# A third buffer for readout weights, a mask added by VectorE, spread bias loads and earlier modulation products in a two-layer hybrid backbone

## The reference

```python
sh1, sc1, g1, sh2, sc2, g2 = split(silu(c) @ w_mod[layer] + b_mod[layer], 6)   # modulation
h = modulate(rmsnorm(x, norm1_g[layer]), sh1, sc1)
...
states = associative_scan(combine, (lam_bar, bu))                              # state-space layer
y = einsum('blgp,ghp->blgh', states, c_re + 1j * c_im).real                    # readout
...
s_loc = einsum('bqhd,bikhd->bhqik', q_row, kb) * scale + bias[None]            # neighbourhood
s_loc = where(col_mask, s_loc, -inf)
p = softmax(concatenate([s_loc, s_ctx]))
...
y = gated_merge([glu(ssm), gqa, na], gates, w_branch, w_out)
```

## Time and profile before

| what | value |
| --- | --- |
| median of 3 runs | 2015.82 us (2014.27 to 2015.94) |
| the profiled execution | 2010.74 us |
| its span, first to last instruction | 2009.1 us |
| TensorE busy | 1714.0 us, 85% |
| VectorE busy | 637.3 us, 32% |
| ScalarE busy | 409.3 us, 20% |
| GpSimdE busy | 347.9 us, 17% |
| mean granted TensorE clock | 0.923 of full speed |

### The profile page before, as it was taken

How to read it: one execution, slowest core, us unless ns; L and a number is a source line. 1 busy time by engine, 2 the same in 40 slices (tenths; PEclk the granted TensorE clock), 3 DMA queues, 4 the chain that set the end, 5 groups by cost and what they waited for, 6 DMA issues and landing times.

```text
span 2009.1 us, 25439 instructions
## 1 busy us (share of the span) xinstructions
PE 1714.0 (85%) x9646; PEld 1049.6 (52%) x9646; DVE 637.3 (32%) x1378; ACT 409.3 (20%) x842; POOL 347.9 (17%) x284
## 2 busy tenths in 40 slices
PE   4999987899999998499979588998879994797794
PEld 1467554454444443355545336755458883464452
DVE  2578642351110113111101367774351112110012
ACT  3111211452000003122212231121242002121122
POOL 0004353681000000100000100435480000000000
PEclk8999986899999999699999788998789997899896
DMA  8411356508412125599999422145703427999992
GB/s 315 149 59 63 122 204 165 164 19 293 168 63 105 67 80 208 210 377 357 384 395 397 145 80 69 43 163 200 166 19 126 168 84 324 341 390 398 399 375 79
DMA packets 104882, 398.33 MB, mean 198 GB/s; under 512 B 43056, under 2 KB 52272, under 8 KB 64336
## 3 DMA queue, kind: packets, MB, share of 16 engines
q1 hardware_dynamic: 46960, 327.01, 41.9%
q10 hardware_dynamic: 50720, 29.54, 6.2%
q0 software_dynamic: 7104, 40.37, 5.9%
HBM read 370.67 MB, written 38.80 MB: 204 GB/s over the span
## 4 chain that ended last, share of the span: by engine, by line
PE 60%; DMA 14%; POOL 7%; DVE 6%; issue 5%; SPq 3%; ACT 3%; ACTq 1%; POOLq 0%; DVEq 0%
PE tile_ps L534 53%; DMA arena<-sorted_in 5%; PE turn_ps L534 4%; SPq L481 3%; DMA ring<-in_wpack 3%; POOL arena L1660 2%; DMA vn<-in_wpack 2%; DMA arena<-in_wpack 2%; PE out_ps L534 1%; DMA sorted_in<-arena,rows 1%; POOL arena L1654 1%; PE turn_ps L749 1%; ACTq L1045 1%; DVE rstd L1316 1%; POOL arena L1645 1%
## 5 line engine op out<-in xcount | busy, mean ns | idle before, releaser
L534 PE MATMUL tile_ps<-h,ring 128*128 128x512 f32 (+1 forms) x1312 | 475.3, 517 | 10.7 <-ACT h L930 8.0
L534 PEld LDWEIGHTS tile_ps<-h,ring 128*128 128x128 f32 x1312 | 250.6, 193 | 221.1 <-issue 206.0
L534 PE MATMUL tile_ps<-arena 64*16 64x128 f32 (+4 forms) x2032 | 244.2, 359 | 37.2 <-POOL arena L1645 16.5
L534 PE MATMUL tile_ps<-arena,ring 128*128 128x512 f32 (+1 forms) x704 | 235.3, 486 | 2.7 <-issue 2.7
L534 PEld LDWEIGHTS tile_ps<-arena 128*64 128x64 f32 (+3 forms) x2032 | 170.9, 161 | 94.1 <-issue 51.3
L534 PEld LDWEIGHTS tile_ps<-arena,ring 128*128 128x128 f32 x704 | 133.6, 190 | 96.6 <-issue 87.6
L1660 POOL TENSOR_SCALAR arena<-arena,smx 128x512 f32<-128x512 f32 (+1 forms) x96 | 127.9, 1349 | 86.8 <-DVE smx L1520 86.4
L534 PE MATMUL tile_ps<-ring,arena 128*64 128x256 f32 (+1 forms) x624 | 101.5, 469 | 9.9 <-ACT arena L1131 7.2
L1684 POOL DMA_DIRECT2D arena<-sorted_in x40 | 20.4, 511 | 515.7 <-PE tile_ps L834 515.7
L1112 ACT ACTIVATE arena<-tile_ps 128x512 f32<-128x512 f32 (+1 forms) x56 | 27.5, 491 | 347.4 <-PE tile_ps L534 347.4
L1581 DVE TENSOR_TENSOR arena<-tile_ps,arena 64x256 f32<-64x256 f32 x40 | 16.7, 417 | 228.2 <-ACT arena L1128 228.2
(11 more groups left out here) (258 smaller groups left out, 2157.2 us busy)
## 6 DMA issues: line engine op xcount, KB each, us to landing
ring<-in_wpack SPq DMA_DIRECT2D x176, 1024.0 KB, 7.9
arena<-in_wpack SPq DMA_DIRECT2D x64, 1024.0 KB, 28.8
h<-in_wpack SPq DMA_DIRECT2D x20, 1024.0 KB, 27.9
qa<-in_wpack SPq DMA_DIRECT2D x12, 1024.0 KB, 14.4
qn<-in_wpack SPq DMA_DIRECT2D x12, 1024.0 KB, 16.6
kn<-in_wpack SPq DMA_DIRECT2D x12, 1024.0 KB, 18.6
vn<-in_wpack SPq DMA_DIRECT2D x12, 1024.0 KB, 21.0
arena<-sorted_in POOLq DMA_DIRECT2D x42, 256.0 KB, 7.6
```

What stands on the lines that cost most here:

```text
L534: return nc.tensor.matmul(out, lhsT, rhs, start=start, stop=stop)
```

## The change

1. The readout weights get a third buffer, `q % 3`; GpSimdE waits for `y(q-3)`.
2. The `qn` projections of iterations 1, 2, 3, 4 go to iterations 1, 3, 5, 7.
3. Modulation blocks 0 and 1 of layer 1 go from attention steps 3 and 7 to iteration 8 of layer 0's readout loop, ahead of `y(7)`; blocks 2 and 3 go from steps 11 and 15 to steps 1 and 2.
4. The mask is added by VectorE in two parts of four additions each (128x512), at the end of steps 14 and 15 in layer 0, 6 and 7 in layer 1. GpSimdE's two additions go, and with them the wait at each masked pair.
5. ScalarE issues the bias loads of layer 0 in steps 0, 2, 4, 6 and the output loads in steps 8, 10, 12, 14; in layer 1 the bias loads stay in steps 0 to 3 and the output loads go to steps 4 to 7, one in each.

```diff
-EVERY = 4
+EARLY = {1: 2, 2: 3}
...
-    return fill[IN_LOOP:IN_LOOP + 2] if q == 0 else fill[IN_LOOP + 1 + q:IN_LOOP + 2 + q]
+    return [fill[IN_LOOP + n] for n, at in enumerate((0, 0, 1, 3, 5, 7)) if at == q]
...
+            names += mod_jobs(l + 1, range(2)) if q == NQ and l + 1 < LAYERS else []
...
+        cp = [cp_first, cp_second, cp_third]
...
+                    if q == NQ and l + 1 < LAYERS:
+                        for n in range(2):
+                            modulation(l + 1, n, l)
+                            modulation_columns(l + 1, n)
...
-                    if n < GRID_H:
-                        load_bias(l, n)
-                    if n == GRID_H:
+                    line = n // 2 if l == 0 and n % 2 == 0 else n if l else None
+                    if line in range(GRID_H):
+                        load_bias(l, line)
+                    if line in range(GRID_H, GRID_H + KW):
...
+                    part = n - len(us) // 2 + 2
+                    if 0 <= part < 2:
+                        dve.wait_ge(bias_in, 16 * GRID_H * (l + 1))
+                        for h2 in range(0, HEADS, 2):
+                            b = bias[:, part, h2:h2 + 2]
+                            b = b.rearrange("p h r c -> p (h r) c")
+                            link(TT(b, b, spread(c("far_cols"), 1, 2 * GRID_H), ALU.add))
...
-                    if q >= 2:
-                        wait_full(pool, (l, "yb", q - 2))
-                        wait_full(pool, (l, "y", q - 2))
+                    if q >= 3:
+                        wait_full(pool, (l, "yb", q - 3))
+                        wait_full(pool, (l, "y", q - 3))
...
-                    if n == 3 * len(us) // 8:
-                        pool.wait_ge(bias_in, 16 * GRID_H * (l + 1))
-                        for qt in range(2):
-                            b = bias[:, qt].rearrange("p h r c -> p (h r) c")
-                            TT(b, b, spread(c("far_cols"), 1, HEADS * GRID_H), ALU.add).then_inc(bias_done, 1)
```

More of the change, by code:

```diff
@@ L216, in tile_jobs @@
             names += [(l, "sc", u, 0), (l, "sc", u, 1)] if u < n_pairs else []
-            if l + 1 < LAYERS and u % EVERY == EVERY - 1 and u // EVERY < MOD1:
-                names += mod_jobs(l + 1, [u // EVERY])
+            names += mod_jobs(l + 1, [EARLY[u]]) if l + 1 < LAYERS and u in EARLY else []
         for kind, *at in mix_order():
@@ L331, in backbone @@
         wtmp, a1 = cut(a1, [GQ, STEP, GRP])
-        cp, a2 = cut(a0, [2, 2 * GQ, NPOS, GRP])
+        cp_first, a2 = cut(a0, [2, GQ, NPOS, GRP])
+        cp_second, a2 = cut(a2, [2, GQ, NPOS, GRP])
+        cp = [cp_first, cp_second, cp_third]
         ctmp, a2 = cut(a2, [GQ, NPOS, GRP])
@@ L738, in _ @@
                                                         qq[a:a + HD, q0:q0 + P], kk[a:a + HD, 0:nk]))
-                    early = l + 1 < LAYERS and n % EVERY == EVERY - 1 and n // EVERY < MOD1
+                    early = l + 1 < LAYERS and n in EARLY
                     if early:
-                        modulation(l + 1, n // EVERY, l)
+                        modulation(l + 1, EARLY[n], l)
                     if LAG <= n < len(us) + LAG:
@@ L1045, in _ @@
                             act.dma_start(tm[j * GRP:(j + 1) * GRP, q % 2], zs[:, :, a:a + P]).then_inc(tm_in, 16)
+                    if q == NQ and l + 1 < LAYERS:
+                        for n in range(2):
+                            copy_rows(l + 1, n)
                     if q:
@@ L1079, in _ @@
                             .then_inc(turn_free[1], 1)
-                    if n < GRID_H:
-                        load_bias(l, n)
-                    if n == GRID_H:
-                        act.wait_ge(y_out, 16 * (l + 1))
-                        for t in range(KW):
-                            act.dma_start(yt[:, t].rearrange("p (j c) -> p j c", j=STEP),
-                                          y_dram[:, t].rearrange("j p c -> p j c")).then_inc(y_in, 16)
-                    if l + 1 < LAYERS and n % EVERY == EVERY - 1 and n // EVERY < MOD1:
-                        copy_rows(l + 1, n // EVERY)
+                    line = n // 2 if l == 0 and n % 2 == 0 else n if l else None
+                    if line in range(GRID_H):
+                        load_bias(l, line)
+                    if line in range(GRID_H, GRID_H + KW):
+                        t = line - GRID_H
+                        act.wait_ge(y_out, 16 * (l + 1))
+                        act.dma_start(yt[:, t].rearrange("p (j c) -> p j c", j=STEP),
+                                      y_dram[:, t].rearrange("j p c -> p j c")).then_inc(y_in, 16)
+                    if l + 1 < LAYERS and n in EARLY:
+                        copy_rows(l + 1, EARLY[n])
                     B = n - LAG - 2
@@ L1472, in _ @@
                         carry_in(q)
+                    if q == NQ and l + 1 < LAYERS:
+                        for n in range(2):
+                            modulation_block(l + 1, n)
                     if q:
```

19 lines of the change are left out of this document (9 added, 10 removed).

## The result

The changed kernel is slower: 2020.8 us against 2011.5 us in the medians of 20 executions of each, ratio 1.0048, 95% interval 1.0024 to 1.0071. In a second comparison (12 and 17 executions) it was 1.0024, 0.9998 to 1.0051. So it is some 5 to 10 us slower, where 6 faster was forecast. Executions of one kernel lie up to 30 us apart here, so I read where the time went in the traces, by stretches of TensorE's timeline, and how much it was in the ratios.

The account below looks back on a forecast made before the run. It took TensorE's waits for GpSimdE's readout weights, plus ScalarE's DMA issues and GpSimdE's mask in attention, as bounds. Loops +16.5 and -1.2, attentions -17.6 and -7, gate +3.1 gave -6.2: 2009.6 us, range 1996 to 2025.

Parts of the forecast that it names:

- Scan beside a third set: Readout loops: making weights 2 during VectorE's scan slows the scan, +5.3 us in layer 0, the same in layer 1.
- What ends an iteration last: Readout loops without GpSimdE waits: VectorE ends layer 0's iterations 2 and 4 (14.6 us), ScalarE's copy iteration 6 (11.0).
- Starved ring: Moved projections delay weight loads: modulation products stall in iterations 4 and 8; layer 1's first gate waits +3.1 us.
- The clock: Readout loops: z and y of iterations 3, 5, 7 may start at the low clock; 2 us each, +6 per layer.
- Attention of layer 0: Steps 0 to 16: blocks, slow loads and mask leave, additions come; 55.1 us against 72.7, -17.6.
- Attention of layer 1: GpSimdE is the bound and loses its mask; about 56.5 us against 63.5, -7.
- (b): Rival, loops: clock falls before each of iterations 3, 5, 7, 4.4 us instead of 2; +14.4, 2024.0 us; chance 0.20.
- (d): Rival, layer 0 attention: ScalarE's issues stay slow, steps 0 to 8 keep 38.0 us; +8.5, 2018.1 us; chance 0.12.
- (a): Rival, loops: the clock stays up; 12 us less, 1997.6 us; chance 0.20.
- (c): Rival, attention: VectorE's mask additions collide with GpSimdE, 8 us more in each layer; +16, 2025.6 us; chance 0.08.
- 2 us or 3.0 in six places: Low-clock cost in iterations 3, 5, 7 of both layers: 2 us forecast; at 3.0 each the whole gain is used up.

Follow-up runs that it names:

- e9: Changed kernel plus unneeded dense products cut to fit TensorE's holes ahead of rope(0) and between halves of stalled modulation products; 2007.2 us, ratio 0.9965 to the kernel before.
- e1: Changed kernel with GpSimdE starting the third set of readout weights only after TensorE has done rope(0); ratio 1.0001 to the kernel before.
- e8: Changed kernel plus unneeded dense products ahead of rope(0) and between halves of stalled modulation products, twice as long as the holes; 2017.0 us, ratio 1.0019.
- e12: Kernel before the change with only ScalarE's bias and output loads spread over the attention steps; ratio 0.9944 to the kernel before.
- e2: Changed kernel with the four qn projections put back in iterations 1, 2, 3, 4; ratio 0.9965 to the kernel before.
- the best one: Kernel before with the change's attention part, third buffer held until rope(0), and unneeded dense products in iterations 5 to 8; 1969.1 us, ratio 0.9782.

## Why the prediction was wrong

The waits and stalls it named are all in the trace; y(7) of layer 0 came 28.8 us later than before (23.2 without the start), not 10 to 17. The sum had the wrong sign because one term of it, the clock in the loops, was half of what it measures.

- **Scan beside a third set: right in size, short of its tail.** +5.3 us in each layer forecast; z(0) to rope(0) grew by 5.6 (220.43 - 195.46 against 19.41) and 4.8. Left out was what comes behind: TensorE has waited 4.3 us, and iteration 1 takes 3.1 us more than before in layer 0 and 1.6 in layer 1, at a lower clock.
- **What ends an iteration last: right in layer 0.** Iteration 2 took 15.0 (14.6 forecast), bound by VectorE as forecast though the clock was at 0.77, iteration 6 10.5 (11.0) at full clock.
- **Starved ring: right.** Stalls of 5.0 to 5.1 us in the iterations named, 5.7 forecast; iteration 8 took 16.75, 14.9 forecast, at a clock of 0.58; the gate wait 2.16 for 3.1.
- **The clock: the step that failed.** "I take 2", in iterations 3, 5 and 7, "+6 in each layer". Iterations 2 to 7 took 98.3 us against my 91.4 at full clock in layer 0, and 90.0 against 78.9 in layer 1: 6.9 and 11.1. Iteration 1 adds 3.1 and 2.5 (in layer 1 it took 1.6 more than before although the 0.9 of waiting is gone), iteration 8 1.9: 11.9 and 13.6 where 6 and 6 stood. With 25.5 in place of 12 the sum is +7 us instead of -6. (Not all of layer 1's is the clock: y(5) waits 0.76 us for DMAs, and iteration 2 ends on a copy of ScalarE that I did not expect.)

  The 2 itself was not too small. Iterations 3, 5 and 7 ran 5.2 us over in layer 0 and 4.5 in layer 1; z and y in them took 7.46, 7.12, 5.89 and 7.91, 7.16, 5.89. What failed is the list of what pays. Iterations 1, 2, 4, 6 and 8 stood at nothing and cost 6.7 and 9.1 us: I charged only iterations that follow one without a projection, though the new waits ahead of rope(0) and in iterations 4 and 8, which are in my own sum, stop TensorE as long. And I charged only z and y, though mr, mc and the mean squares behind them double too (3.64 for 1.92, 1.87 for 1.05, 2.07 for 1.12).

  e9 agrees from the other side: filling just those holes, with no wait of the engines or loads taken away, returns 12 to 17 us by the ratios, as much as I had set for all of it or more. Only 6.4 of them stand in the loops of its one trace; where the rest fell is open, and so is how the loss divides between stops and small products that turn slow without one (e1, e8).
- **Attention of layer 0: right.** Steps 0 to 4 took 16.7 us (17.5), 4 to 8 11.6 (12), 8 to 12 10.5 (10.8), 12 to 16 10.5. The additions fall behind step 16, where 3.4 us show (waits of 1.10 and 2.32 us for VectorE), so 12 to 16 with them is 13.9 (14.8).
- **Attention of layer 1: right**, -6.8 for -7 (the terms of the text, 50.3 + 2 + 4.5, add up to 56.8, not 56.5).

Of the rivals, (b) names the cause, the clock, but not its places: it wanted 4.4 us in z and y of iterations 3, 5 and 7, which lost 2.0 at most. That 2020.8 lies 3.2 us from its 2024.0 is luck; (d)'s 2018.1, whose mechanism is out, is nearer still. (a), the clock stays up, is what e8 and e9 bring about in part. (c) is out as a price: mask additions take 0.68 to 1.09 us, 0.76 in the median, beside GpSimdE's scaling, while the scan's take up to 2.02 beside its products. The rule of the Trainium skill ("SBUF — State Buffer", Who interferes with whom), by which both pairs collide, agrees with the scan. Of the mask the trace shows a small effect only, with the scaling at 1.85 us at most where it was 1.58 before. (d) is out: the four spread bias loads of layer 0 were issued in 0.60 to 0.71 us each, and e12 gained by them. In layer 1, where they were not spread, the fourth still took 4.17.

So the wrong decision was not the one the text weighed, 2 us or 3.0 in six places: those six measured 1.6 each. It was to price every new wait at its length alone and to look for the low clock only where a projection had left; the rows it went by were of loops with dense projections in four iterations in a row, which the change takes apart.

## What to carry to other kernels

Where TensorE's work is small products, price a wait at its length and what follows it: here most stops of 2 us and more were followed by products at up to twice their time, 1.2 to 4.4 us in z and y alone (7.12 to 10.27 instead of 5.89). Some products lose it without a stop, so closing a wait does not bring all of it back. Spreading dense work thin may cost the same way; e2 undid that and gained, but it removed three stalls at once, so its share is not shown. Cheap dense filler in a hole that can't be closed wins part of it back (12 to 17 us in the changed kernel, some 19 in the best one). And before a loader's order is changed, list which job gives back the slot that each load needs: three stalls of 5 us and one of 2 were plain in that list.

## What was not expected of the hardware

- Products whose result nobody reads made the kernel faster: 1969.1 us with 9 of them in each layer's loop, 1987.9 without.
- How much a stop costs differs between executions of one kernel (in layer 1, z and y behind a wait of 2.56 us took 7.93, behind one of 2.41 us 10.27), and the start of the kernel alone differs by up to 11 us with the granted clock of 40 to 80 us. Both spread the runs; how much of the 30 us they make is not shown.
- Small products ran at up to twice their time right behind a fully busy stretch as well (mr 3.64 us in e1, 3.40 in e8, 3.36 before).
- One execution of the version with filler took 4528 us, TensorE at about 0.4 of its speed while its granted clock is recorded as 1.0; the others of that kernel, 12 in two sessions, 1965 to 1981. What caused it is open.
